# GpSimd takes one weight split and one quarter of the first norm's low parts from VectorE

## What is computed

```
mod = silu(c) @ w_ada + b_ada                      # 2048 -> 6 x 2048
sh1, sc1, ga1, sh2, sc2, ga2 = split(mod, 6)
h = rms_norm(x, g_norm1) * (1 + sc1) + sh1
qa, ka, va, oa, gates, qb, kb, vb = split(h @ w_in)
```

## Time and profile before

| | |
|---|---|
| median of 3 runs | 2371.89 us (2370.17 to 2371.92) |
| profiled execution | 2370.85 us |
| its span (first to last instruction) | 2369.0 us |
| TensorE busy | 2326.4 us, 98% |
| VectorE busy | 1895.6 us, 80% |
| GpSimd busy | 5.7 us, 11 instructions |
| first stage, up to the fourth weight piece's first matmul | 118.3 us |
| granted TensorE clock, mean | 0.994 |

### The profile page before, as it was taken

How to read it: one execution, slowest core, us unless ns; L and a number is a source line. 1 busy time by engine, 2 the same in 40 slices (tenths; PEclk the granted TensorE clock), 3 DMA queues, 4 the chain that set the end, 5 groups by cost and what they waited for, 6 DMA issues and landing times.

```text
span 2369.0 us, 32294 instructions
## 1 busy us (share of the span) xinstructions
PE 2326.4 (98%) x13232; PEld 2025.4 (85%) x13232; DVE 1895.6 (80%) x2144; ACT 1138.0 (48%) x1431; POOL 5.7 (0%) x11
## 2 busy tenths in 40 slices
PE   5899999999999999999999999999999999999999
PEld 3588888889888888888889888898888888989987
DVE  6888898899888778889768787887887666886754
ACT  2253445547555334555446444644555334665552
POOL 0000000000000000000000000000000000000000
PEclk9899999999999999999999999999999999999999
DMA  9989777785777788878765788866777774674343
GB/s 396 364 332 351 277 290 274 246 297 178 278 279 271 249 272 292 290 280 289 247 209 191 280 320 317 289 241 243 281 279 272 279 273 168 226 274 150 125 168 135
DMA packets 119011, 620.23 MB, mean 262 GB/s; under 512 B 13392, under 2 KB 14672, under 8 KB 76112
## 3 DMA queue, kind: packets, MB, share of 16 engines
q1 hardware_dynamic: 70560, 446.40, 53.3%
q10 hardware_dynamic: 48304, 171.76, 19.5%
HBM read 616.01 MB, written 2.10 MB: 261 GB/s over the span
## 4 chain that ended last, share of the span: by engine, by line
PE 93%; DVE 4%; DMA 2%; issue 0%; ACT 0%; SPq 0%; DVEq 0%; ACTq 0%
PE pm L647 25%; PE pm L648 13%; PE ps L647 13%; PE ps L648 6%; PE pm L705 5%; PE pm L706 5%; PE pm L707 5%; PE ps L705 2%; PE ps L706 2%; PE ps L707 2%; DVE acc_first L1848 2%; PE pm L662 1%; PE pm L661 1%; PE pm L663 1%; DMA e<-in_ada 1%; DMA ada<-in_ada 1%
## 5 line engine op out<-in xcount | busy, mean ns | idle before, releaser
L1782 DVE TENSOR_TENSOR w_lo<-raw,w_hi 128x2048 fp32r<-128x2048 f32 (+2 forms) x412 | 892.1, 2166 | 329.3 <-ACT w_hi L1219 328.0
L1219 ACT ACTIVATE w_hi<-raw 128x2048 fp32r<-128x2048 f32 (+2 forms) x412 | 747.6, 1815 | 545.3 <-DMA raw<-in_w_down 112.1
L647 PE MATMUL pm<-h,w_hi 128*128 128x512 f32 x1534 | 529.7, 391 | 1.5 <-DVE w_lo L1782 0.7
L648 PE MATMUL pm<-h,w_lo 128*128 128x256 f32 x1534 | 424.4, 277 | 0.0
L1794 DVE SCALAR_TENSOR_TENSOR acc<-ada,csil,acc 128x1024 f32<-128x1024 f32 x300 | 384.0, 1280 | 1.5
L647 PEld LDWEIGHTS pm<-h,w_hi 128*128 128x128 f32 x1534 | 288.0, 188 | 63.6 <-issue 3.2
L648 PEld LDWEIGHTS pm<-h,w_lo 128*128 128x128 f32 x1534 | 288.0, 188 | 0.2
L647 PE MATMUL ps<-h,w_hi 128*128 128x512 f32 x786 | 271.8, 391 | 0.0
L648 PE MATMUL ps<-h,w_lo 128*128 128x256 f32 x786 | 217.4, 277 | 0.0
L647 PE MATMUL pm<-h_sgu,w_hi 128*128 128x512 f32 x608 | 209.1, 391 | 0.0
L647 PEld LDWEIGHTS ps<-h,w_hi 128*128 128x128 f32 x786 | 147.6, 188 | 31.4 <-issue 0.7
(11 more groups left out here) (512 smaller groups left out, 4088.4 us busy)
## 6 DMA issues: line engine op xcount, KB each, us to landing
ada<-in_ada ACTq DMA_DIRECT2D x320, 512.0 KB, 5.7
raw<-in_w_up SPq DMA_DIRECT2D x88, 1024.0 KB, 5.0
raw<-in_w_in SPq DMA_DIRECT2D x56, 1024.0 KB, 5.5
raw<-in_w_down SPq DMA_DIRECT2D x64, 704.0 KB, 4.8
raw<-in_sgu_u SPq DMA_DIRECT2D x32, 1024.0 KB, 5.4
raw<-in_sgu_v SPq DMA_DIRECT2D x32, 1024.0 KB, 5.2
raw<-in_sgu_z SPq DMA_DIRECT2D x32, 1024.0 KB, 4.9
raw<-in_sgu_out SPq DMA_DIRECT2D x32, 1024.0 KB, 4.9
```

Of the source, the lines that this page charges most:

```text
L647: pe.matmul(dst[:, :], wh[:, k, :], hl, start=(kc == 0), stop=False, skip_group_check=True)
L648: mm = pe.matmul(dst[:, 0:T], wl[:, k, :], hi, start=False, stop=last, skip_group_check=True)
L1219: act.activation(hi_(q, n), raw_(q, n), ACT.Copy).then_inc(hi_ready, 1)
L1782: tt_(lo_(q, n), raw_(q, n), whole(hi_(q, n)), ALU.subtract).then_inc(lo_ready, 1)
```

## The change

The third piece's low split (`split(2)`) and the low parts of chunks 4 to 7 (`first_low(1)`) are taken out of VectorE's list. GpSimd gets them as its first work: it waits for two low splits (`lo_ready` 2) and three high splits (`hi_ready` 3), makes the third low split, and then for each chunk of 4 to 7 adds the shift to `nt` in place (a `tensor_scalar`, new) and takes the high part away (a `tensor_tensor`), with a wait on its own semaphore `xn_shifted` between them. VectorE's one operation per chunk becomes two on GpSimd. VectorE waits for the third `lo_ready` at the end of the stage. The counts of all semaphores stay as they were.

```diff
--- before.py
+++ after.py
@@ -103,7 +103,7 @@
 K_DVE = [[k for k in range(KC) if k not in K_PE[q]] for q in range(QUARTERS)]
 N_PE = [sum(len(K_PE[i]) for i in range(q)) for q in range(QUARTERS + 1)]
 N_DVE = [sum(len(K_DVE[i]) for i in range(q)) for q in range(QUARTERS + 1)]
-FIRST_SPLITS = [(1, 11), (2, 1), (2, 10)]
+FIRST_SPLITS = [(1, 11), (2, 1)]
 FIRST_USED = N_DVE[QUARTERS]
 ADA_SPANS = [("ka", 4, 12, 18), ("va", 0, 8, 14), ("qb", 0, 16, 28), ("vb", 0, 15, 24), ("w_out", 0, 9, 12),
              ("w_up0", 6, 37, 32), ("w_down0", 0, 32, 18), ("w_up1", 0, 44, 42), ("w_down1", 0, 12, 4), ("sgu_v", 0, 32, 40),
@@ -371,6 +371,7 @@
         std_ready = sem("std_ready")
         rstd_ready = sem("rstd_ready")
         xn_ready = sem("xn_ready")
+        xn_shifted = sem("xn_shifted")
         hh_ready = sem("hh_ready")
         h_ready = sem("h_ready")
         x_ready = sem("x_ready")
@@ -1762,6 +1763,16 @@
         @block.gpsimd
         def _(pool):
 
+            q = len(FIRST_LOADS) - 1
+            pool.wait_ge(lo_ready, q)
+            pool.wait_ge(hi_ready, q + 1)
+            n = elems(q)
+            pool.tensor_tensor(lo_(q, n), raw_(q, n), whole(hi_(q, n)), ALU.subtract).then_inc(lo_ready, 1)
+            for kc in range(4, 8):
+                pool.wait_ge(hh_ready, kc + 1)
+                pool.tensor_scalar(nt[:, kc % 4, :], nt[:, kc % 4, :], mod(SH1, kc), None, ALU.add).then_inc(xn_shifted, 1)
+                pool.wait_ge(xn_shifted, kc - 3)
+                pool.tensor_tensor(h[:, kc, T:2 * T], nt[:, kc % 4, :], whole(h[:, kc, 0:T]), ALU.subtract).then_inc(h_ready, 1)
             for p in range(PAIRS - 1):
                 pool.wait_ge(pre_sq, p + 1)
                 buf = pre_bufs[p % 4]
@@ -1966,13 +1977,14 @@
                     if q and k == 4:
                         first_xn(q - 1)
                         take(q - 1, 0)
-                    if q and k == 7:
+                    if q and q != 2 and k == 7:
                         first_low(q - 1)
                     if (q, k) in FIRST_SPLITS:
                         split(FIRST_SPLITS.index((q, k)))
             first_xn(QUARTERS - 1)
             take(QUARTERS - 1, 0)
             first_low(QUARTERS - 1)
+            dve.wait_ge(lo_ready, len(FIRST_LOADS))
 
 
             G = slice(0, GROW)
```

## The result

The changed kernel is slower by 0.6%: 2388.89 us in the median of 8 runs (2380.86 to 2399.27), against 2372.84 for the kernel before, run beside it; ratio 1.0064, interval 1.0046 to 1.0081. The profiled execution has a span of 2389.2 us, 20.3 more than before.

A forecast was written before the change was run, and what follows sets the result against it. It took TensorE to bound the kernel, with the first stage limited by VectorE's sums and transfers nearly alike. 2370.85 + 13.1 (later take) - 1.6 (coming back) = 2382.35, plus 1.04 to the median: 2383; range 2379 to 2387 (0.55).

The forecast's parts named there:

- GpSimd's split: First stage: GpSimd's third low split takes 4.45 us, until 78.8; a VectorE sum stands still behind it and ends at 79.9.
- The alternation: GpSimd's eight small operations take turns with VectorE's sums, 1.40 us behind a shift, 1.68 behind a low part; done at 90.6.
- The rival of a shift that runs free: The one-input shift needs no turn with VectorE: low parts at 85.5, kernel 2378; chance 0.16 together with no exclusion.
- TensorE: From chunk 7's low part to VectorE's take: gate products 0.5, column part 2.7, row piece 3.6 at half clock, then 5.3 us.
- Transfers: SyncE's piece 52 waits for the late row piece's buffer: issued at 97.4 instead of 81.06, landing about 3.6 us later.
- VectorE by itself: VectorE loses 4.0 us by the split and 4 x 0.29 by low parts, against 3.8 saved: 1.4 us.
- What comes back: Stage's end: TensorE, without pause at full clock, regains 0.6 in the turn and 1.4 at the column part, less 0.45: 1.6 us.
- exclusion missing: Rival: GpSimd and VectorE do not exclude each other, 2377 (chance 0.16), or 2374 if the clock also stays at 2.4 GHz (0.06).
- in time: Rival: GpSimd at VectorE's prices has chunk 7's low part by 80.6, no transfer late, 0.5 us gained; chance 0.03.
- The dearer GpSimd: Rival: split of 5.9 us and small operations of 1.0 us give 2388, at 1.4 us each 2391; chance 0.2.

The follow-up runs named there:

- low parts only: Changed kernel with the third low split back on VectorE, GpSimd making only the four low parts; median 2377.74 us, ratio 1.0019 to the kernel before.
- second execution: The changed kernel, unaltered, run and profiled once more against the kernel before; median 2387.10 us against 2375.01, ratio 1.0055.
- the row ahead: Changed kernel with TensorE's piece 44 row piece and quarter 2 turn ahead of gate and column products; median 2376.98 us, ratio 1.0017 to the kernel before.
- low parts first: Changed kernel with GpSimd making the low parts before the split; median 2380.70 us, ratio 1.0030 to the kernel before.
- fourth row piece: Kernel before, with one more piece of the last quarter (k = 12) on TensorE instead of VectorE; median 2376.00 us, ratio 1.0008.
- run 2: Not a run label: part of the phrase "run 2 to 3% slower", said of stretches of the weight stream; no kernel or measurement has this name.

## Why the prediction was right

The forecast was 2383, with 2376 to 2391 around it; the medians are 2388.9 and 2387.1, or by the ratios and the 2371.89 shown first 2387 and 2385. 2383 would be a ratio of 1.0047, inside both intervals, though near the lower end of the first. The narrower 2379 to 2387, which was given 0.55, is missed by the medians by 1.9 and 0.1 us. The chain of causes held; of its terms some were off:

- **GpSimd's split** was to hold from 74.3 to 78.8; VectorE let go at 74.1 (0.13 before 74.24) and it ended at 78.59: 4.48 us, predicted 4.45. The stopped sum ended at 79.68 (79.9).
- **The alternation.** Sums of 1.31 us behind a shift and 1.56 behind a low part, which by the prediction's 0.13 and 1.08 us is a hold of 0.46 and 0.71 (predicted 0.45 and 0.73), and a chunk took 3.08 us (81.66 - 78.58), as predicted. The last low part ended at 91.36 instead of 90.6. The term that was wrong is the half microsecond that VectorE's `tensor_scalar` of k = 0 was to save: it cost 0.9 instead. Chunk 6 took 3.94 us (88.67 - 84.73): the operation itself 0.96 instead of 0.75, the shift beside it 2.23 instead of 1.89, and the low part behind them stood through a whole sum, 1.64 instead of 1.13. The last small operation found VectorE's sums done and came 0.4 sooner than reckoned. The rival of a shift that runs free falls: a chunk would have taken 1.68 us. With the low parts only, a shift's row lasts 1.48, 1.89 or 2.96 us, and ends 0.93 after what would be its turn each time, so the rest is waiting.
- **TensorE.** Predicted 0.5 + 2.7 + 3.6 + 5.3 us from the low part to the take; measured 0.86 + 2.70 + 2.17 + 5.10. The mis-sized term is the row piece: the clock came back within it (granted at 1.00 from 95.6 us). It offset the late low part, and the take stood at 102.19 (predicted 102.7). The second execution had 2.60 and 6.62 there, 2.0 us more in sum, for the same program: this part isn't fixed to better than that.
- **Transfers.** Issue at 97.12 (97.4), landing 3.5 us later (3.6). The share was 0.01 and 0.00 from 85 to 95 us.
- **VectorE by itself** loses 1.8 us instead of 1.4, as the kernel with the row ahead shows. The stopped sum costs 3.9, three sums 0.3 each behind low parts, the `tensor_scalar` 0.2, and the shifts and a wait for a piece 0.2 together. What was saved is 3.4 and not 3.8: the prediction counted from start to start, and left out the 0.1 us that stands between two sums in any case.
- **What comes back** was to be 1.6 and is 1.1. The turn and the column part returned 0.57 + 1.17, but VectorE needed 16.62 us from the take to its last sum instead of 15.95: it waited 0.76 for piece 55 (106.41). The prediction had that wait at nothing: it let the pieces land every 1.28 us after piece 52, the last at 115.1, "ahead of its use". But piece 54 landed 3.2 us behind piece 53 (105.11 after 101.91), and piece 63 at 117.38, only 0.15 before VectorE's last sum began. So at the end of the stage the transfers were again as late as VectorE. The prediction also counted TensorE late by 0.45, where it was 0.75 early.

The stage's +11.5 came out as forecast because two errors of half a microsecond cancel (the take at +12.6 for +13.1, the return 1.1 for 1.6); the second execution, at +12.9, shows that TensorE's clock alone moves this sum by more than that. Inside the take, too, the late low part (+0.8) and the fast row piece (-1.4) cancel in part. That is luck, not precision. The medians lie 4 to 6 above the forecast. The kernel before, beside them, stood 1.0 and 3.1 above the median that the forecast started from; the rest is of the size of TensorE's clock (1.4) and of the slow stretches, but that they make it up in the median isn't shown.

Of the rivals, exclusion missing is refuted by the stopped sums, and "in time" by 91.36 against the 80.6 that it needed. The dearer GpSimd came near the median, but not by its mechanism: split and small operations cost what was forecast.

## What to carry to other kernels

Before work is given to an idle engine, ask what stands behind its result in the order of the engine that waits: here 8.9 of the 11.5 us came from a row piece that frees a transfer buffer and stood behind the late operand in TensorE's list. Two moves that cost 2.7 and 2.8 us alone cost 11.5 together. The low parts alone came 9.1 us late and used up the 3.6 us that TensorE had in hand; the split in front of them on GpSimd made them 7.6 us later still, and nothing was left to hide it.

And a GpSimd operation that reads SBUF beside two-input VectorE operations holds VectorE up. VectorE lost 3.9 us to a hold of 4.5, and 2.2 to an addition of 2.4, but only 0.3 to one of 0.7 and 0.03 to a shift. The shorter the hold, the smaller the share of it that VectorE lost. The split relieved VectorE of 2.0 us and took 3.9.

## What the runs showed of the hardware

- GpSimd's `tensor_scalar` of 128 x 256 lasts about 0.93 us from its turn (its span of 1.89 begins in the wait), yet by the working above it lets VectorE go after 0.46; the `tensor_tensor` of the same size lasts 0.72 and lets go after 0.71. The sum of VectorE behind them took 1.31 and 1.56 us instead of 1.28.
- VectorE's `tensor_scalar` of 128 x 1024, with one tensor input, also took its turn with GpSimd: 0.96 us instead of 0.75 beside a shift that took 2.23 instead of 1.89 (1.21 us beside a `tensor_tensor`, with the low parts first).
- The granted clock fell behind 3.7 us of one-column matmuls in which TensorE never paused (fourth row piece, 0.58 of full speed on average from 109 to 113 us), and a second time soon after it had come back (low parts first, 0.50 from 92 to 102 us; the changed kernel again, 0.50 from 99.9 to 103.2). Whether it falls there isn't fixed: the same program had 5.10 and 6.62 us in the same place.
- At a granted clock of 1.00 whole stretches of the weight stream, up to some 250 us long, run 2 to 3% slower: 232 to 233 ns instead of 227 from the start of a 512-column matmul to the next start (the group's mean duration is 395 instead of 389 ns). They come at the same places of the program, in some executions only.
